# Joining two norms over the same x, and the small steps around them, in a float32 two-block transformer kernel on one Trainium2 core

## The reference, cut to what matters

```
h  = x + mix @ w_out                       # end of layer one, x is 512 x 1024
y  = h  / sqrt(mean(h*h)  + eps) * final_g # final norm of layer one; the residual stream of layer two
n  = y  / sqrt(mean(y*y)  + eps) * attn_g  # input norm of layer two
q, k, v, mq = n @ w_in_diff                # 6 heads: q and k of 128 columns, v of 128; memory query of 256
bias[h, i, j] = table[bucket(j - i), h]    # table is 32 x 6
memory: kv = norm(mem) * gain_i @ w_mem_i, for both upper layers (i = 0, 1)
```

## Time and profile before

| | |
|---|---|
| median of 3 runs | 1934.56 us (1932.63 to 1938.84) |
| profiled execution, its own time | 1933.61 us |
| span of that execution in the profile | 1931.8 us |
| PE busy | 1803.0 us, 93% of the span |
| POOL, DVE, ACT busy | 704.1, 955.4, 542.9 us |
| layer two's opening, as traced | out1 ends at 590.7 us, unit 0 of the attention begins at 740.5 us, its last turn is at 914.9 us |

### The profile page before, as it was taken

One profiled execution on the slowest core, in us unless ns is written; L12 is line 12 of the kernel. 1 busy time (PEld: TensorE's weight loads), 2 busy tenths in 40 slices (PEclk: granted clock), 3 DMA queues, 4 the chain that ended last, 5 costly groups with the idle time before them and its releaser, 6 DMA issues.

```text
span 1931.8 us, 28399 instructions
## 1 busy us (share of the span) xinstructions
PE 1803.0 (93%) x11800; PEld 1444.1 (75%) x11800; DVE 955.4 (49%) x1645; ACT 542.9 (28%) x1090; POOL 704.1 (36%) x333
## 2 busy tenths in 40 slices
PE   8999888889788988986999999999999899999999
PEld 5688667777676676764888888887777588888887
DVE  6675256566644434555566654123345266555411
ACT  3111112344423154545322221003422332222100
POOL 4333100000243311321655555454323275555542
PEclk9999999998898899998999999998999899999999
DMA  5222210000131411210322233331112133332222
GB/s 175 66 87 94 65 45 3 3 2 2 35 122 63 136 36 58 68 53 22 97 93 97 97 99 98 98 99 60 55 57 67 41 100 98 99 97 95 94 96 77
DMA packets 43205, 142.48 MB, mean 74 GB/s; under 512 B 5267, under 2 KB 7077, under 8 KB 42950
## 3 DMA queue, kind: packets, MB, share of 16 engines
q1 hardware_dynamic: 43078, 140.67, 22.3%
HBM read 136.06 MB, written 4.06 MB: 73 GB/s over the span
## 4 chain that ended last, share of the span: by engine, by line
PE 50%; DVE 2%; ACT 2%; issue 1%; POOL 1%; DMA 0%; DVEq 0%; SPq 0%; ACTq 0%
PE b_p_bank L206 16%; PE b_p_bank L208 15%; PE b_p_bank L207 15%; PE b_p_bank L2559 0%; PE b_p_bank L2554 0%; POOL b_wlo L187 0%; PE b_p_bank L2541 0%; DVE l_sc L2183 0%; PE b_p_bank L1890 0%; DVE l_mx L2189 0%; PE b_p_bank L1866 0%; PE b_p_bank L2498 0%; PE b_p_bank L2497 0%; DVE l3t_ke L2672 0%; DMA gate_w<-in_gate_w 0%
## 5 line engine op out<-in xcount | busy, mean ns | idle before, releaser
L187 POOL TENSOR_TENSOR b_wlo<-b_raw,b_whi 128x1024 fp32r<-128x1024 f32 x238 | 582.6, 2451 | 830.7 <-DVE b_whi L180 830.7
L206 PE MATMUL b_p_bank<-b_hi,b_whi 128*128 128x512 f32 x1008 | 407.4, 404 | 7.6 <-PEq L71 6.6
L180 DVE CAST b_whi<-b_raw 128x1024 fp32r<-128x1024 f32 x238 | 182.2, 773 | 457.6 <-PE b_p_bank L208 388.0
L208 PE MATMUL b_p_bank<-b_hi,b_wlo 128*128 128x512 f32 x1008 | 397.1, 394 | 0.0
L207 PE MATMUL b_p_bank<-b_lo,b_whi 128*128 128x512 f32 x1008 | 397.1, 394 | 0.0
L206 PEld LDWEIGHTS b_p_bank<-b_hi,b_whi 128*128 128x128 f32 x1008 | 192.0, 191 | 52.9 <-issue 13.4
L207 PEld LDWEIGHTS b_p_bank<-b_lo,b_whi 128*128 128x128 f32 x1008 | 192.1, 191 | 40.8 <-issue 2.6
L208 PEld LDWEIGHTS b_p_bank<-b_hi,b_wlo 128*128 128x128 f32 x1008 | 191.9, 190 | 41.0
L206 PE MATMUL b_p_bank<-f_mhi,b_whi 128*128 128x512 f32 x352 | 136.9, 389 | 0.0
L207 PE MATMUL b_p_bank<-f_mlo,b_whi 128*128 128x512 f32 x352 | 136.9, 389 | 0.0
L208 PE MATMUL b_p_bank<-f_mhi,b_wlo 128*128 128x512 f32 x352 | 136.9, 389 | 0.0
(11 more groups left out here) (428 smaller groups left out, 3106.4 us busy)
## 6 DMA issues: line engine op xcount, KB each, us to landing
b_raw<-in_w_up SPq DMA_DIRECT2D x88, 512.0 KB, 3.6
b_raw<-in_w_down SPq DMA_DIRECT2D x44, 512.0 KB, 3.6
b_raw<-in_w_in SPq DMA_DIRECT2D x32, 512.0 KB, 3.6
b_raw<-in_w_out SPq DMA_DIRECT2D x24, 512.0 KB, 3.6
b_raw<-in_w_gla SPq DMA_DIRECT2D x22, 512.0 KB, 3.7
b_raw<-in_w_diff SPq DMA_DIRECT2D x20, 512.0 KB, 3.7
b_raw<-in_w_mem SPq DMA_DIRECT2D x8, 512.0 KB, 3.7
all_x<-in_x SPq DMA_DIRECT2D x8, 256.0 KB, 6.0
```

The source lines that it names most:

```text
L180: self.nc.vector.tensor_copy(self.hi[:, n % SLOTS, :], self.raw[:, n % RAWS, :]).then_inc(self.s_hi, 1)
L187: self.nc.gpsimd.tensor_tensor(self.lo[:, n % SLOTS, :], self.raw[:, n % RAWS, :], self.hi[:, n % SLOTS, :].bitcast(F32), ALU.subtract).th ...
L206: nc.tensor.matmul(acc, lhsT=left[0], rhs=right[0], start=first, stop=False)
L208: return nc.tensor.matmul(acc, lhsT=left[1], rhs=right[0], start=False, stop=last)
```

## The change

Three things change, and the plan of layer two is written anew.

- `Opening` becomes `MemoryNorm` (four steps, memory only), and `JoinedNorm` takes both norms from the same unscaled x. For each block ACT takes the square of x and the square of x * final_g, and PE sums both, into two banks: 16 squares and 16 sum products, as many as before. hi and lo are made from x with the product of both gains, two blocks a step in steps 4 to 7. DVE forms sum2 + eps * sum1 (two operations). ACT takes the logarithm of both, then the exponential of both. DVE scales x by final_g and the first root at the end, two blocks in each of steps 10 to 13.
- `Bias` multiplies the table [32, 6] by the bucket matrix once, in two pieces, which gives all six heads on six partitions. DVE copies them into `row` [6, 640]. Each head's scratch line is written by one transfer that reads its one row of `row` 128 times. All six are issued in step 1 of Bias, and the first three strips are read back in step 3. Bias has 4 steps instead of 9.
- The v tiles of a pair of heads come behind q and k of the second head instead of the first; so q5 and k5 come ahead of the last v. The projection begins with bank 2.

By the new plan the bias' steps lie among those of mk1, the memory keys' steps among those of mk1, mv1 and mq, and the memory attention begins at q0.1. Counted from unit 0 to unit 18 there are 49 steps of projection (V01.7 to V45.7) and 5 of row0; behind unit 18 there are 8 of row0.

```diff
+class JoinedNorm:
+    n = KD + 2 + 4
+    def scalar(self, act):
+        for j in range(KD):
+            if j == KD // 2:
+                act.wait_ge(self.s_both, 2)
+                act.wait_ge(self.s_free, self.free_at)
+            act.wait_ge(self.s_x, j + 1)
+            if j >= KD // 2:
+                for i in (2 * j - KD, 2 * j - KD + 1):
+                    nc.scalar.activation(self.hi[:, i, :], self.x[:, i, :], ACT.Copy, scale=self.both[:, i:i + 1]
+                                         ).then_inc(self.s_hi, 1)
+            nc.scalar.activation(self.sq1[:, j % 2, :], self.x[:, j, :], ACT.Square).then_inc(self.s_sq1, 1)
+            nc.scalar.activation(self.sq[:, j % 2, :], self.x[:, j, :], ACT.Square, scale=self.final[:, j:j + 1]
+                                 ).then_inc(self.s_sq, 1)
+            yield
+        act.wait_ge(self.s_t, 2)
+        nc.scalar.activation(self.rstd[:, :], self.rstd[:, :], ACT.Ln, scale=1.0 / D, bias=self.tiny[:, 0:1]
+                             ).then_inc(self.s_ln, 1)
+        nc.scalar.activation(self.r1[:, :], self.banks[0][:, :], ACT.Ln, scale=1.0 / D, bias=self.k["eps"][:, 0:1]
+                             ).then_inc(self.s_l1, 1)
+        nc.scalar.activation(self.rstd[:, :], self.rstd[:, :], ACT.Exp, scale=-0.5).then_inc(self.s_rstd, 1)
+        nc.scalar.activation(self.r1[:, :], self.r1[:, :], ACT.Exp, scale=-0.5).then_inc(self.s_r1, 1)
+        yield
...
+    def vector(self, dve):
...
+        dve.wait_ge(self.s_sum1, KD)
+        nc.vector.tensor_scalar(self.r1[:, :], self.banks[0][:, :], EPS, None, ALU.mult).then_inc(self.s_t, 1)
+        dve.wait_ge(self.s_t, 1)
+        dve.wait_ge(self.s_ss, 1)
+        nc.vector.tensor_tensor(self.rstd[:, :], self.banks[1][:, :], self.r1[:, :], ALU.add).then_inc(self.s_t, 1)
+        yield
+        yield
+        dve.wait_ge(self.s_r1, 1)
+        for j in range(KD):
+            nc.vector.scalar_tensor_tensor(out=self.x[:, j, :], in0=self.x[:, j, :], scalar=self.final[:, j:j + 1],
+                                           in1=self.r1[:, :], op0=ALU.mult, op1=ALU.mult).then_inc(self.s_xn, 1)
+            if j == KD - 1:
+                dve.wait_ge(self.s_xn, KD)
+            if j % 2:
+                yield
...
 class Bias:
...
-        self.row, self.lv = shelf.sb("row", [P, 2, REL]), shelf.sb("lv", [1, 2, 2, HD])
+        self.row, self.lv = shelf.sb("row", [DH, REL]), shelf.sb("lv", [1, 2, 2, HD])
     def put(self, sp, h):
-        sp.wait_ge(self.s_row, 2 * h + 2)
-        sp.dma_start(self.line[h, :, :], self.row[:, h % 2, :]).then_inc(self.s_line[h % 2], 16)
+        src = self.row[h:h + 1, :].unsqueeze(1).broadcast_to([1, P, REL])
+        sp.dma_start(self.line[h:h + 1, :, :], src).then_inc(self.s_line[h], 16)
     def sync(self, sp):
         yield
-        for h in range(DH + 2):
-            if h >= 1 and h - 1 < DH:
-                self.put(sp, h - 1)
-            if 3 <= h < 6:
-                self.fetch(sp, h - 3)
-            yield
+        sp.wait_ge(self.s_row, 2)
+        for h in range(DH):
+            self.put(sp, h)
+        yield
+        yield
+        for h in range(3):
+            self.fetch(sp, h)
+        yield
     def tensor(self, pe):
+        pe.wait_ge(self.i_t, 16)
         pe.wait_ge(self.i_b, 16)
-        pe.wait_ge(self.s_sp, 1)
         pe.wait_ge(*self.banks_free)
-        for h in range(DH):
-            for n, (a, b) in enumerate(self.parts):
-                if h >= 1:
-                    pe.wait_ge(self.s_row, 2 * h - 1 + n)
-                self.nc.tensor.matmul(self.ps[n][:, 0:b - a], lhsT=self.spread[:, h, :], rhs=self.bucket[:, a:b],
-                                      start=True, stop=True).then_inc(self.s_b, 1)
-            yield
+        for n, (a, b) in enumerate(self.parts):
+            self.nc.tensor.matmul(self.ps[n][0:DH, 0:b - a], lhsT=self.table[:, :], rhs=self.bucket[:, a:b],
+                                  start=True, stop=True).then_inc(self.s_b, 1)
+        yield
         pe.wait_ge(self.s_d, 2)
         self.nc.tensor.matmul(self.pl, lhsT=self.k["ones"][0:1, :], rhs=self.dot[:, :],
                               start=True, stop=True).then_inc(self.s_pl, 1)
...
 def second_layer(u, kt1, vt1):
...
+    proj.turn = 2
...
-        if h % 2 == 0:
-            v = proj.tokens(n, before, 0, TT, vt[:, :, P * h:P * h + 2 * P], tcol)
+        if h % 2:
+            v = proj.tokens(n, before, 0, TT, vt[:, :, P * (h - 1):P * (h + 1)], tcol)
...
-    plan = [0] + [1] * 16 + [1] * 6 + spread(10, 7)
-    plan += [1, 0] * 4 + [0] + spread(26, 8)
-    plan += [1] * 9 + [0] + [1] * 3 + [0]
...
+    plan = [0] + [1] * 22 + [0] + [1] * 2 + [0] + [1] + [0] + [1, 0] * 4 + [1] * 3
+    plan += [1] * 3 + [0, 1] * 4 + [1] + [0]
+    plan += [1] * 6 + [0] + [1, 0] * 4 + spread(6, 4) + spread(6, 2) + [1] * 2
...
```

More of the change, by code:

```diff
@@ L1547, in split @@
                                       scale=self.mem_gains[i][:, j:j + 1]).then_inc(self.s_hi, 1)
[L1549 to L1553, removed]
     def scalar(self, act):
@@ L1575, in scalar @@
         yield
-        for j in range(KD):
-            self.square(act, j)
-            yield
[L1579 to L1583, removed]
-        yield
     def low(self, dve, i):
@@ L1603, in vector @@
         yield
[L1604 to L1610, removed]
         yield
@@ L1634, in tensor @@
             pe.wait_ge(self.s_sq, j + 1)
-            nc.tensor.matmul(self.bank[:, :], lhsT=self.k["ones"][:, :], rhs=self.sq[:, j % 2, :], start=(j == 0),
-                             stop=(j == KD - 1)).then_inc(self.s_ss, 1)
+            nc.tensor.matmul(self.banks[1][:, :], lhsT=self.k["ones"][:, :], rhs=self.sq[:, j % 2, :], start=(j == 0),
+                             stop=(j == KD - 1)).then_inc(self.s_sum if j < KD - 1 else self.s_ss, 1)
             yield
         yield
+        pe.wait_ge(self.s_rstd, 1)
@@ L1641 @@
+        for t in range(TT):
+            mm = nc.tensor.matmul(self.col_bank[:, t:t + 1], lhsT=self.rstd[0:1, t * P:t * P + P],
+                                  rhs=self.k["ones"][0:1, 0:1], start=True, stop=True)
+        mm.then_inc(self.s_ct, 1)
+        yield
 class Bias:
-    n = DH + 3
+    n = 4
     def __init__(self, nc, tag, k, shelf, strip, lam, banks, small, banks_free):
@@ L1656, in __init__ @@
         self.ps, self.pl, self.banks_free = banks, small, banks_free
-        (self.i_t, self.i_b, self.i_l, self.s_b, self.s_row, l0, l1, self.s_d, self.s_pl, self.s_e, self.s_end,
-         self.s_sp) = sems(nc, tag, "it", "ib", "il", "b", "row", "line0", "line1", "d", "pl", "e", "end", "spread")
-        self.s_line = [l0, l1]
+        (self.i_t, self.i_b, self.i_l, self.s_b, self.s_row, self.s_d, self.s_pl, self.s_e, self.s_end) = sems(
+            nc, tag, "it", "ib", "il", "b", "row", "d", "pl", "e", "end")
+        self.s_line = sems(nc, tag, *(f"line{h}" for h in range(DH)))
         self.s_strip = sems(nc, tag, *(f"strip{h}" for h in range(DH)))
@@ L1705, in vector @@
         nc, lv, lam = self.nc, self.lv, self.lam
-        dve.wait_ge(self.i_t, 16)
-        nc.vector.tensor_copy(self.spread[:, :, :], self.table[:, :].unsqueeze(2).broadcast_to([RB, DH, P])
-                              ).then_inc(self.s_sp, 1)
         dve.wait_ge(self.i_l, 16)
@@ L2172, in combine @@
             if n == 0:
-                for i in range(2):
-                    dve.wait_ge(self.bias.s_line[i], 16 * (DH // 2))
+                for i in range(DH):
+                    dve.wait_ge(self.bias.s_line[i], 16)
             if t == 0:
@@ L2962, in second_layer @@
                        sqb.rearrange("p j (b t) -> p (j b) t", b=2)[:, 0:2, :], S[2], free)
-            for i, (t, at, free) in enumerate(((kt, at_k0, (opening.s_ln, 1)), (kt1, at_k1, None)))]
+            for i, (t, at, free) in enumerate(((kt, at_k0, (opening.s_r, 1)), (kt1, at_k1, None)))]
+    keys[0].sq_free = (before.s_sum1, KD)
     keys[1].bank_free, keys[1].sq_free = (keys[0].s_ln, 1), (keys[0].s_out, 1)
```

100 lines of the change are left out of this document (70 added, 30 removed).

## The result

The changed kernel takes 1966.81 us (median of 4 runs, 1962.15 to 1967.36) against 1934.32 us (1932.63 to 1938.84, 4 runs) for the kernel before, run beside it: a ratio of 1.0159 with a 95% interval of 1.0136 to 1.0182. It is slower by 32 us. The forecast was 1912; rival 2, the one-partition writes, came true, at 1972 by its own working.

The account below looks back on a forecast made before the run. PE, busy 93% of the span, was taken as the bound; -8.0 - 6.8 - 4.4 - 1.6 - 2.1 = -22.9 us from 1933.6 gave 1910.7, 1911.7 against the median. Forecast 1912, own range 1902 to 1922, 8-in-10 range 1898 to 1985.

Parts of the forecast that it names:

- rival 2: One-partition scratch-line writes choke the load queue, PE loses 60.5 us before the query sums: 1972 us, slower; chance 0.41.
- T: Time per head's 320 KB scratch-line write from one partition: bounds 2.0 to 15.8 us, fast value taken for the forecast.
- 6 T - 10.9: Microseconds PE loses before the query sums behind six line writes; nothing at T = 2.0, eats the gain from 5.6.
- A: Joined norm: the chain in front of the ones product at 607.18 and slow clock behind it go, gain 8.0 us.
- B: Bias: one product pair saves 15.6 us, new lambda wait costs 6.7 and slow clock 2.1; net -6.8 us.
- Rival 3: Scalings of x don't meet POOL's work, so no wait at lambda: 8.8 us less, 1903 us; chance 0.14.
- C: Key norms spread over mk1 to mq: 7.6 us gone, new query-sum wait 1.2 and other costs; net -4.4 us.
- D: A V01 step between roots and unit 0 cuts the gap there from 3.79 to 2.2 us: -1.6 us.
- E: Row0 no longer waits for k5 but about 4 us for ACT's copies of the last v: -2.1 us.
- F: Rest of the attention: moved dense steps fill some idle time but lose cover; taken as 0, between -4 and +7.
- rival 4: ACT's and DVE's chain sets the attention's pace: F = +7 and E = 0 give 1921 us; chance 0.10.
- Rival 5: Gains and new waits cancel, with T of about 4 to 6 us: 1935 us; chance 0.04.

Follow-up runs that it names:

- HBM rows: Changed kernel, but the six bias rows go once to HBM and each head's line is written from its row there: 1907.25 us, ratio 0.986.

## Why the prediction was wrong, point by point

- **The step that failed** is the choice of T: "I take the fast value for the forecast, since each kind of transfer seen here lands in 2.3 to 3.7 us, but only by a little." T is 12.19 us in the kernel, 13.6 with its landing when measured alone. The rows it leaned on all have 128 partitions at their SBUF end, so they said nothing of a source of one. Of its bounds, 2.0 and 15.8 us, it took the lower one, though even their middle, 8.9, lies over the 5.6 us from which T decides, and though its own chances stood at 0.41 for rival 2 and 0.31 for the forecast. The 11.9 us of rival 2 met the size, but its reckoning by the pace of one to two transfer engines was luck: all 16 were busy to 0.87 to 0.91 while the lines ran, and the source was the limit. The page of the Trainium skill weighed beside it, "SBUF — State Buffer", section "Door 1: The DMA port swizzle", had the mechanism as well as the size (12 us a head, an estimate).
- **Rival 2's own working held.** 6 T - 10.9 is 62.2 us at T = 12.19; the gap is 58.7, and HBM rows are 58 us faster. With them the kernel takes 1907 where the forecast for a fast T said 1912. Its signs came as named: writes 12 us apart, a cast released by a transfer, one gap of tens of us in front of the query sums. Only the tile landed at 709.8, not near 700. What the working left out: SP was to wait for the third line, and in fact the issues themselves hold it from the third line on.
- **A.** No gap stands between mk0's first step and the column of roots, as said. The 8.0 us were not tried alone. (The sum counts 1.06 + 2.14 us of slow clock behind this stop, and only 2.1 behind the larger one of B, "as in A".)
- **B.** The pair took 1.24 us for 1.3. The bias alone won 14.5 for 15.6. The lambda gap is 6.60 for 6.7, with its cause as named: DVE's second four scalings 6.91 us, two of them beside POOL. Rival 3 is out. That gap was worth 3.6 us and not 6.7 + 2.1, since what follows then waits for wlo. So B won 10.9 (14.5 - 3.6) for 6.8: the price of the lambda wait was set too high.
- **C, D.** Key gaps gone, the query sums wait 1.52 (for 1.2), unit 0 2.44 (for 2.2). In front of unit 0 25.6 us were won for a sum of 20.8. Of this B has 10.9, if its two parts add up, and A, C and D the other 14.7, for 14.0. Their sum is about right; how it falls to the three was not tried.
- **E, F.** Row0 waits 1.91 us in its second step for ACT's copies of v, for 4. From unit 0 on 1.7 us were won, for 2.1. But the reason was off: with the old order of v and the new plan row0 waits 0.55, so k5 is no hindrance any more. The new order of v wins some 8 us by idle time and clock all through the attention. With the new plan and the old order that stretch is 183.7 us long in its trace, longer than the 174.4 of before. With 1.7 us won from unit 0 on, F's +7 of rival 4 did not come. Rival 5 was out at this T.

## What to carry to other kernels

Ask of every transfer how many partitions its SBUF end reaches, not only how many bytes it has: 320 KB took 2.2 us from 128 partitions and 13.6 from one, and a pace under 30 GB/s while such a transfer runs is its sign on the page. The DMA share is not: it was 0.93 for one partition and 0.23 for four at that same pace. If one row must be written many times, put it once to HBM and copy from there (4.1 us, and 15 KB first). On a queue that also carries the weights, price such a transfer by what PE can do without the next tile: the same six cost 58 us in one order and 34 in another. And a bound whose middle lies beyond the deciding point is a forecast, not a footnote.

## What the runs showed of the hardware that was not expected

- An issue on SP's queue is not free once slow transfers are outstanding: two were taken in 0.6 us each, the third held SP for 9.25 us, each later line for 12.15, and in the kernel with three such lines the first two lines from HBM behind them held SP for the same 12.15 us each. In the changed kernel SP waited for no semaphore in that time. Why the third is the first to be held stays open.
- Two one-partition transfers took some 23 to 25.6 us, in one queue or in two, from one group of four partitions or from two. Within one transfer two groups gave 49 GB/s.
- With the bias alone and one-partition rows PE stopped for 8.78 us in the middle of a step, with no releaser: "issue". From the queues between 711 and 713 us, near the end of that stop:

```profile
q8 instruction: 1, 0.02, 2.9%
```

An instruction transfer began there at 712.0 to 712.2 us, and PE went on at 714.24. That PE's instructions came late behind the lines fits this, but it was not tried apart.
